# Copies of the k projection moved from VectorE to ScalarE, and more conditioning rows summed by VectorE in the front of a one-core decoder layer

## The reference

```python
c_act = jax.nn.silu(c)
ada = c_act @ w_ada[l] + b_ada[l]                     # 1024 x 6144
shift1, scale1, gate1, shift2, scale2, gate2 = jnp.split(ada, 6, axis=-1)
h = modulate(rms_norm(x, norm1_g[l]), shift1, scale1)
# token_mixer: proj = h @ w_in, columns zu, zv (gating unit), q, k, v (attention), f (forgetting)
z_u, z_v = gelu(proj[..., :512]), gelu(proj[..., 512:1024])
# spatial_gating: per-head LayerNorm of z_v, then the position mixing, times z_u
# forgetting_attention: softmax(q k^T / 8 + F_t - F_s) v, causal, F a running sum of log sigmoid(f)
y = jnp.concatenate([head_rms_norm(y_sg, ...), head_rms_norm(y_fox, ...)], axis=-1)
x = x + gate1[:, None, :] * (y @ w_out)
h = modulate(rms_norm(x, norm2_g[l]), shift2, scale2)
x = x + gate2[:, None, :] * peer_ffn(h, ...)          # top-16 of 16384 experts for each of 8 heads
return rms_norm(x, final_g)
```

## Time and profile before

| | us |
|---|---|
| median of 3 runs | 1682.81 |
| lowest and highest | 1677.38, 1685.94 |
| profiled execution, whole | 1684.25 |
| its span, first to last instruction | 1682.5 |
| TensorE busy | 1583.2 (94%) |
| VectorE busy | 1257.5 (75%) |
| ScalarE busy | 685.3 (41%) |
| GpSimd busy | 389.0 (23%) |

### The profile page before, as it was taken

How to read it: one execution, slowest core, us unless ns; L and a number is a source line. 1 busy time by engine, 2 the same in 40 slices (tenths; PEclk the granted TensorE clock), 3 DMA queues, 4 the chain that set the end, 5 groups by cost and what they waited for, 6 DMA issues and landing times.

```text
span 1682.5 us, 23151 instructions
## 1 busy us (share of the span) xinstructions
PE 1583.2 (94%) x7853; PEld 1340.8 (80%) x7853; DVE 1257.5 (75%) x2278; ACT 685.3 (41%) x1247; POOL 389.0 (23%) x326
## 2 busy tenths in 40 slices
PE   6997788999999999999989999899999999999995
PEld 6585665555569998999989999898788888878884
DVE  3668354549948988899888988458788888878887
ACT  2421132312238842587337853233333333333333
POOL 1000030000003310033001346314333334334430
PEclk9898889999999999999999999899999999999998
DMA  8755430000228984499646999978999999999982
GB/s 301 275 188 214 147 139 1 1 1 1 85 88 315 368 319 138 154 366 362 241 138 248 359 390 412 393 281 300 369 345 334 361 360 343 346 346 348 344 316 88
DMA packets 172900, 425.77 MB, mean 253 GB/s; under 512 B 13324, under 2 KB 62476, under 8 KB 169624
## 3 DMA queue, kind: packets, MB, share of 16 engines
q1 hardware_dynamic: 86528, 265.37, 42.5%
q0 software_dynamic: 36864, 134.23, 21.9%
q10 hardware_dynamic: 49432, 25.19, 5.3%
HBM read 372.32 MB, written 52.43 MB: 252 GB/s over the span
## 4 chain that ended last, share of the span: by engine, by line
PE 77%; DVE 9%; DMA 7%; issue 2%; ACT 2%; POOL 1%; ACTq 1%; SPq 0%; DVEq 0%; POOLq 0%
PE bank L1172 9%; PE bank L1173 9%; PE bank L1174 9%; PE bank L1227 9%; PE bank L1228 9%; PE bank L1231 9%; PE bank L1118 7%; PE bank L1187 5%; PE bank L1101 3%; DMA weights<-gates_dense 2%; DMA weights<-in_expert_v 2%; PE bank L1015 2%; DVE ada L1280 1%; POOL weights L596 1%; DVE u_lo L1595 1%
## 5 line engine op out<-in xcount | busy, mean ns | idle before, releaser
L1172 PE MATMUL bank<-h_hi,u_hi 128*128 128x384 f32 x1024 | 351.5, 343 | 21.3 <-DVE u_lo L1595 13.6
L1174 PE MATMUL bank<-h_hi,u_lo 128*128 128x384 f32 x1024 | 345.6, 338 | 0.0
L1173 PE MATMUL bank<-h_lo,u_hi 128*128 128x384 f32 x1024 | 345.5, 337 | 0.0
L1227 PE MATMUL bank<-v_hi,w_hi 128*128 128x512 f32 x768 | 299.4, 390 | 4.3 <-DVE w_lo L1702 4.2
L1228 PE MATMUL bank<-v_lo,w_hi 128*128 128x512 f32 x768 | 298.9, 389 | 0.0
L917 ACT ACTIVATE v_hi<-weights 128x1024 fp32r<-128x1024 f32 x128 | 135.8, 1061 | 331.4 <-PE bank L1231 261.3
L1231 PE MATMUL bank<-v_hi,w_lo 128*128 128x512 f32 x768 | 236.5, 389 | 0.0
L1698 DVE TENSOR_TENSOR v_lo<-weights,v_hi 128x1024 fp32r<-128x1024 f32 x128 | 157.6, 1231 | 95.4 <-ACT v_hi L917 94.9
L1595 DVE TENSOR_TENSOR u_lo<-weights,u_hi 128x1024 fp32r<-128x1024 f32 x128 | 156.1, 1223 | 96.5 <-PE bank L1174 81.8
L1172 PEld LDWEIGHTS bank<-h_hi,u_hi 128*128 128x128 f32 x1024 | 195.2, 191 | 24.5 <-DVE u_lo L1595 13.2
L1173 PEld LDWEIGHTS bank<-h_lo,u_hi 128*128 128x128 f32 x1024 | 195.4, 191 | 0.0
(11 more groups left out here) (275 smaller groups left out, 2302.3 us busy)
## 6 DMA issues: line engine op xcount, KB each, us to landing
weights<-in_uT SPq DMA_DIRECT2D x128, 512.0 KB, 6.0
weights<-in_expert_v SPq DMA_DIRECT2D x128, 512.0 KB, 6.3
gates_dense<-weights SPq DMA_DIRECT2D x24, 1024.0 KB, 7.6
weights<-gates_dense ACTq DMA_DIRECT2D x16, 1536.0 KB, 27.8
shared<-gelu_dense SPq DMA_DIRECT2D x64, 384.0 KB, 7.6
shared<-in_w_ada SPq DMA_DIRECT2D x16, 1024.0 KB, 5.3
gelu_dense<-weights SPq DMA_DIRECT2D x32, 384.0 KB, 5.9
gelu_dense<-ada SPq DMA_DIRECT2D x32, 384.0 KB, 4.8
```

Source lines behind the costliest of these rows:

```text
L1172: nc.tensor.matmul(a, uh[:, k, :], h2_hi[:, :, k, :], start=(k == 0), stop=False)
L1173: nc.tensor.matmul(a, uh[:, k, :], h2_lo[:, :, k, :], start=False, stop=False)
L1174: ins = nc.tensor.matmul(a, ul[:, k, :], h2_hi[:, :, k, :], start=False, stop=(k == KC - 1))
L1227: nc.tensor.matmul(acc, wh, v_hi[:, r % 2, cols], start=begin, stop=False)
```

## The change

`SUMMED_K` becomes a value per group: 5 for groups 0 and 1 and 7 for groups 2 and 3, so VectorE sums two blocks more of each of the latter, and TensorE one in place of three. The load of group 3 is issued as two DMAs of four blocks, the first with a semaphore of its own (`half_in`); VectorE begins group 3 on the first half, and waits for the second ahead of block 4. The copies of the k banks leave VectorE, where they stood behind the norm of z_v, and stand on ScalarE behind `round_in("q")`. The place of the norm itself, behind the remainders of q, is the same in both kernels.

```diff
-SUMMED_K = 5
+SUMMED_K = (5, 5, 7, 7)
...
-            load_group("ada", 3)
+            last = EARLY_ADA - 1
+            sp.dma_start(weights[:, slot_of["ada", last], 0:KC // 2, :], group_source("ada", last)[:, 0:KC // 2, :]).then_inc(half_in, 16)
+            sp.dma_start(weights[:, slot_of["ada", last], KC // 2:KC, :], group_source("ada", last)[:, KC // 2:KC, :])\
+                .then_inc(weight_in[slot_of["ada", last]], 16)
...
             round_in("q")
+            for n in range(4):
+                b = wait_full(act, "k", n)
+                release(nc.scalar.activation(kT[:, n, :], b[:, :], ACT.Copy), "k", n)
             for g in range(8, 10):
                 ada_row(g)
...
-                    for k in range(SUMMED_K, KC):
+                    for k in range(SUMMED_K[g], KC):
...
-                w = wait_weights(dve, "ada", g)
+                if g == EARLY_ADA - 1:
+                    dve.wait_ge(half_in, 16)
+                    w = weights[:, slot_of["ada", g], :, :]
+                else:
+                    w = wait_weights(dve, "ada", g)
                 acc = ada[:, g * HALF:(g + 1) * HALF]
-                for k in range(SUMMED_K):
+                for k in range(SUMMED_K[g]):
+                    if g == EARLY_ADA - 1 and k == KC // 2:
+                        wait_weights(dve, "ada", g)
...
-            for n in range(4):
-                b = wait_full(dve, "k", n)
-                release(nc.vector.tensor_copy(kT[:, n, :], b[:, :]), "k", n)
             b = wait_full(dve, "cum")
```

More of the change, by code:

```diff
@@ L326, in program @@
         x_in, c_in, small_in, norm1_in = sem("x_in"), sem("c_in"), sem("small_in"), sem("norm1_in")
+        half_in = sem("half_in")
         late_in = [sem(f"late_in{b}") for b in range(LATE)]
@@ L985, in ada_cols @@
                     at = g * 4 + j
-                    for k in range(SUMMED_K, KC):
+                    for k in range(SUMMED_K[g], KC):
                         nc.tensor.matmul(cols[:, 16 + at:17 + at], w[:, k, j * P:(j + 1) * P], c_act[:, k:k + 1],
-                                         start=(k == SUMMED_K), stop=(k == KC - 1))
+                                         start=(k == SUMMED_K[g]), stop=(k == KC - 1))
                 pe.wait_ge(ada_summed, g + 1)
@@ L1264, in ada_sum @@
             def ada_sum(g):
-                w = wait_weights(dve, "ada", g)
+                if g == EARLY_ADA - 1:
[3 more added lines that the diff above has]
+                    w = wait_weights(dve, "ada", g)
                 acc = ada[:, g * HALF:(g + 1) * HALF]
-                for k in range(SUMMED_K):
+                for k in range(SUMMED_K[g]):
+                    if g == EARLY_ADA - 1 and k == KC // 2:
+                        wait_weights(dve, "ada", g)
                     ins = stt(out=acc, in0=w[:, k, :], scalar=c_act[:, k:k + 1], in1=acc, op0=ALU.mult, op1=ALU.add)
-                    if k < SUMMED_K - 1:
+                    if k < SUMMED_K[g] - 1:
                         link(ins)
```

## The result

The changed kernel takes 1657.51 us (median of 4 runs, 1655.15 to 1660.01), the kernel before 1680.6 (4 runs, 1677.38 to 1685.94). The ratio is 0.986 with a 95% interval of 0.9826 to 0.9893: 23 us less. The profiled execution took 1655.15, with a span of 1653.4.

A forecast was written before the change was run, and what follows sets the result against it. TensorE's 19.5 us wait before q and its column sums in the front were taken as the bound; 18.7 + 1.8 (20.5) plus 4.8 gave 25.3 off the profiled 1684.25, 1658.95, adjusted by 1.4 to 1657.5, range 1651 to 1666.

The forecast's parts named there:

- The bound and its cause: Before q, TensorE waits 19.5 us for VectorE's k bank copies, queued behind the norm, which q doesn't need.
- 18.7 us for the start of q: With k copied by ScalarE, q starts at 156.8, behind its remainders, in place of 175.51.
- 1.8 us of clock, with 0 as the other bound: First nine q matmuls run at full clock, since only a 0.8 us gap precedes them: 1.8 us saved, or 0.
- 4.8 us in the front: Conditioning column sums of groups 2 and 3 on TensorE end at 38.8 in place of 43.65.
- The halves: Group 3's load as two DMAs in the front: cost and gain both put at zero.
- The front's 4.8 passes on: From zv to q, TensorE's work and VectorE's late sums both move earlier together by the 4.8 us.
- rival A: Before q, late sums wait for DMA, so the front's gain is lost: 1662.3 us, chance 0.08.
- The clock in v: When the clock rises again in zv was said to differ by some tenths of a us.
- Nothing else late behind q: Behind q, loads, gating and TensorE's rows follow its end, so the 20.5 us passes on; other delays cost nothing.
- the slack that I gave the norm: VectorE's norm, ready at 174.69, is 3.9 us ahead of q's new end; each microsecond beyond costs one.
- B: At q, the banks gain nothing and only the front counts: 1678.0 us, chance 0.05.
- C: Clock falls to the lower level from q on: q costs 19.5 us more, possibly slower overall; chance 0.02.

The follow-up runs named there:

- after, again: The changed kernel, unedited, run and profiled a second time beside other kernels: 1657.20 us, ratio 0.9857 to the kernel before.
- k only: Changed kernel with the front undone: k copied by ScalarE, five rows summed in every group, group 3 loaded whole; 1658.54 us, ratio 0.9848 to the kernel before.

## Why the prediction was right, and where its terms were off

The forecast was 1657.5 and the median is 1657.51. The closeness is partly luck: the saving was put at 25.3 and is 23.1 by the medians, while the median of before came down by 2.2 with one more run. At the end of q the traces have 23.0 and 22.6 of the 25.3. In the first execution 1.0 went to waits of the late sums and about 1.0 to a slower start of v than in the execution of before, in the second 1.5 to the waits and 1.6 to the clock at the start of q.

- *The bound and its cause.* As told. The wait of 19.5 us was the place of the k copies behind the norm: moved to ScalarE, or ahead of the norm on VectorE, they free q; with another piece of work as long ahead of q it comes back (20.6 us).
- *18.7 us for the start of q.* The step that q would start directly behind its remainders holds (0.05 us behind). Put into one sum with the front it was too large: q starts 21.3 us earlier, not 23.5, and 22.6 in the second execution.
- *1.8 us of clock, with 0 as the other bound.* Both ends were met: q is 21.9 long with the clock kept and 23.5 with it lost, in executions of the same kernel. The gap I counted on was 0.8 us, and with the k copies alone it was 0.90 and the clock was kept. With the front it was 1.8 and 2.2, and in the kernels without halves, with the copies first on VectorE and with the late norm (gaps 1.9, 2.3 and 1.8) the clock fell as well.
- *4.8 us in the front.* 4.71, and by the parts of the sum: the last adding matmuls start at 37.07 (36.9 forecast) and take 1.87 (1.84). The halves were worth nothing, as forecast.
- *The front's 4.8 passes on.* This is the mis-sized term: all of it reaches TensorE's end of k, but only 3.9 us reach the q remainders. How long v runs slowly changes from execution to execution with either front, so executions have to be compared that are alike in it. "Slow" below counts v matmuls that start 0.40 us or more ahead of the next one (0.23 at full clock), "rows behind k" is where these conditioning rows start:

  | kernel | slow | v starts | rows behind k | remainders end |
  |---|---|---|---|---|
  | before | 7 | 83.72 | 154.15 | 156.75 |
  | after, again | 6 | 78.63 | 148.83 | 152.88 |
  | k only | 13 | 83.62 | 155.24 | 157.97 |
  | after | 12 | 78.97 | 150.47 | 154.11 |

  In each pair k ends 4.8 to 5.3 us earlier and the remainders end 3.9 earlier. The difference is in the waits of VectorE's late sums for their loads: 8.3 and 8.4 us together with the old front, 9.8 and 9.3 with the new one. That is the mechanism of rival A, which was thus part of the result rather than an alternative. The clock in v, put at some tenths, is worth more: it moved the end of k by 1.6 us between two executions of the changed kernel, and by 1.1 between the two with the old front.
- *Nothing else late behind q.* Held: 288.5 us from there to the u stream, 288.7 before. But the slack that I gave the norm, 3.9 us, was counted to the end of q. TensorE needs the norm only at 180.2, 8.1 us behind its end in the changed kernel, and what costs when it is late is not that wait: SP's queue reaches the `w_out` loads through a wait for the norm's variance, and 12.6 us of delay cost 7.3 by way of the load and GpSimd. The forecast was not hurt, since 11.6 us lay between the two issues.
- *Rivals.* B is refuted by the trace and by the k copies alone. C, a low clock through all of q, did not happen; the clock fell for a few us in several places in place of one long stretch. No run here bears on a limit of current.

## What to carry to other kernels

When one engine waits long for a small copy, look at what stands ahead of that copy in its queue: moving it ahead of the long work did as much here as moving it to another engine. The next limit is then found by asking what the freed work waits for. Here it was the next piece in the same queue, and putting that ahead of sums wanted only later took the wait out of the trace, though by time that alone could not be told. When executions of one kernel differ by a clock that rises sooner or later, compare those that agree in it before a difference is put down to the edit. Before an engine's work is called off the path, read every queue that waits for it, the DMA-issuing one too.

## What the runs showed of the hardware

TensorE's granted clock did not behave alike behind alike pauses. Behind a wait of 1.81 us the q matmuls stood 0.34 and 0.24 apart and stayed so (q length 21.93); behind one of 2.22 us, in the same kernel, 0.49 and 0.42. With the late norm the wait was 1.80, and yet the clock was lost (23.49). In the kernel without halves the wait was 1.88 and the first four were quick, the fifth already slow:

```profile
153.45 0.50 PE L1039 MATMUL bank<-hT_hi,q_in_hi 128*128 128x512 f32 x1 [1.88 <-DVE q_in_lo L1321]
...
154.49 0.48 PE L1040 MATMUL bank<-hT_lo,q_in_hi 128*128 128x512 f32 x1
154.77 0.63 PE L1041 MATMUL bank<-hT_hi,q_in_lo 128*128 128x512 f32 x1
```

The Trainium skill (TensorE: Matmul & The Clock Gate, section "What's actually happening") says that the gate is set by how busy TensorE has been recently. The q rows do not contradict it, but no run here shows what the gate looks at. For a forecast it means that such a term has two values, 0 and about 1.6 us here. The same holds in the attention, where a fall to a granted clock of 0.51 made one execution of an unchanged stage 3.6 us longer.

The clock also fell while TensorE did not pause at all. In the changed kernel the forgetting logits are 64 matmul rows of 8 columns in a row, from 69.67 to 79.12 us. TensorE is busy all through, yet its granted clock is 1.00 at 73 to 74 us and 0.50, the lower level, from 75:

```profile
69.67 9.45 PE L1028 MATMUL bank<-gate,hT 128*128 128x8 f32 x64
```

```profile
73.00:74.00 1.00, 1.00 (x11) 1.00 (x10) 0.00 (x0) 1.00 (x2) 0.00 (x0) 1.00 1.03 395
...
75.00:76.00 1.00, 1.00 (x7) 1.00 (x6) 0.00 (x0) 0.54 (x1) 0.00 (x0) 0.50 0.04 16
```

With most of them set one by one among the wide matmuls of zv, the clock stays at full where v begins:

```profile
76.00:80.00 4.00, 4.00 (x24) 3.45 (x24) 2.84 (x5) 3.98 (x5) 0.00 (x0) 1.00 0.00 2
```

So a stage in which the profile calls TensorE busy throughout can still lose the clock. Setting these matmuls elsewhere, with the clock kept, brought the end of k 4.7 and 3.0 us forward against the two executions of the changed kernel.
